# Feed-forward of a two-block transformer kernel: which engine makes the low halves of the input's Winograd forms, and where one down weight is split

## The reference

```python
        h2 = rmsnorm(x, norm2_g[l])
        gate = jnp.einsum('bsd,df->bsf', h2, w_gate[l])
        up = jnp.einsum('bsd,df->bsf', h2, w_up[l])
        x = x + jnp.einsum('bsf,fd->bsd', jax.nn.silu(gate) * up, w_down[l])
    return rmsnorm(x, final_norm_g)
```

## Time and profile before

| | |
|---|---|
| median of 3 runs | 3688.02 us (3686.49 to 3693.86) |
| profiled execution, its own time | 3687.42 us |
| its span in the profile | 3685.7 us |
| TensorE busy | 3505.6 us, 95% |
| VectorE busy | 2130.1 us, 58% |
| GpSimd busy | 1732.3 us, 47% |
| ScalarE busy | 1155.6 us, 31% |

### The profile page before, as it was taken

How to read it: one execution, slowest core, us unless ns; L and a number is a source line. 1 busy time by engine, 2 the same in 40 slices (tenths; PEclk the granted TensorE clock), 3 DMA queues, 4 the chain that set the end, 5 groups by cost and what they waited for, 6 DMA issues and landing times.

```text
span 3685.7 us, 51935 instructions
## 1 busy us (share of the span) xinstructions
PE 3505.6 (95%) x22042; PEld 2927.5 (79%) x22042; DVE 2130.1 (58%) x2745; ACT 1155.6 (31%) x1919; POOL 1732.3 (47%) x1248
## 2 busy tenths in 40 slices
PE   8999999988999999999999999989999899999998
PEld 7788878867778787877878888777788777787876
DVE  7845566377364545456774466647778355454454
ACT  2122122267222222223122122336666222222223
POOL 4332333549255555555233323632488345545454
PEclk9999999999999999999999999999999999999999
DMA  3110312554101111113111132362121200101011
GB/s 124 36 41 30 143 64 83 180 143 143 59 23 46 58 46 58 46 57 143 47 35 35 35 149 80 117 203 70 58 92 58 92 23 35 69 35 69 35 69 63
DMA packets 79690, 275.82 MB, mean 75 GB/s; under 512 B 9057, under 2 KB 9313, under 8 KB 76900
## 3 DMA queue, kind: packets, MB, share of 16 engines
q1 hardware_dynamic: 70816, 242.25, 19.6%
q10 hardware_dynamic: 8642, 30.24, 2.2%
HBM read 224.23 MB, written 48.23 MB: 74 GB/s over the span
## 4 chain that ended last, share of the span: by engine, by line
PE 74%; DVE 15%; ACT 4%; POOL 3%; issue 3%; DMA 0%; POOLq 0%; SPq 0%; DVEq 0%; ACTq 0%
PE ps L1426 20%; PE ps L1428 19%; PE ps L1427 19%; PE ps L1432 4%; PE ps L1726 2%; PE ps L1696 2%; PE ps L1697 2%; PE ps L1731 2%; DVE tf_lo_p L2122 2%; DVE acc L2123 1%; DVE af_hi_p L2122 1%; ACT wd_hi L1780 1%; DVE af_lo_p L2122 1%; DVE px L2122 1%; PE ps L1501 1%
## 5 line engine op out<-in xcount | busy, mean ns | idle before, releaser
L2717 POOL TENSOR_TENSOR ring_lo<-ring_raw,ring_hi 128x512 fp32r<-128x512 f32 (+1 forms) x356 | 596.6, 1681 | 381.8 <-ACT ring_hi L1780 372.2
L1426 PE MATMUL ps<-a_hi,ring_hi 128*128 128x512 f32 x1472 | 589.5, 400 | 29.9 <-DVE af_hi_p L2122 16.0
L1428 PE MATMUL ps<-a_hi,ring_lo 128*128 128x512 f32 x1472 | 575.9, 391 | 0.0
L1427 PE MATMUL ps<-a_lo,ring_hi 128*128 128x512 f32 x1472 | 575.8, 391 | 0.0
L1426 PEld LDWEIGHTS ps<-a_hi,ring_hi 128*128 128x128 f32 x1472 | 277.8, 189 | 104.2 <-DVE af_hi_p L2122 23.6
L1428 PEld LDWEIGHTS ps<-a_hi,ring_lo 128*128 128x128 f32 x1472 | 277.6, 189 | 59.9
L1427 PEld LDWEIGHTS ps<-a_lo,ring_hi 128*128 128x128 f32 x1472 | 278.2, 189 | 54.3
L2122 DVE TENSOR_TENSOR xres<-xres,ps 128x512 f32<-128x512 f32 x352 | 234.6, 684 | 147.9 <-PE ps L1428 145.7
L1426 PE MATMUL ps<-wd_hi,af_hi 128*128 128x512 f32 x704 | 277.0, 394 | 24.5 <-DVE xres L2122 18.7
L1780 ACT ACTIVATE ring_hi<-ring_raw 128x512 fp32r<-128x512 f32 (+1 forms) x286 | 180.6, 635 | 308.8 <-PE ps L1428 195.5
L1427 PE MATMUL ps<-wd_lo,af_hi 128*128 128x512 f32 x704 | 275.8, 392 | 0.0
(11 more groups left out here) (305 smaller groups left out, 8055.6 us busy)
## 6 DMA issues: line engine op xcount, KB each, us to landing
ring_raw<-w SPq DMA_DIRECT2D x92, 512.0 KB, 3.6
ring_raw<-wgu SPq DMA_DIRECT2D x68, 512.0 KB, 3.7
uq<-q_scr SPq DMA_DIRECT2D x96, 256.0 KB, 4.7
ring_raw<-wd SPq DMA_DIRECT2D x34, 512.0 KB, 3.6
ring_raw<-wo SPq DMA_DIRECT2D x32, 512.0 KB, 3.6
uk<-k_scr SPq DMA_DIRECT2D x6, 2048.0 KB, 10.5
rlf<-wgu SPq DMA_DIRECT2D x20, 512.0 KB, 4.5
xraw<-xt SPq DMA_DIRECT2D x16, 512.0 KB, 7.4
```

The lines of the kernel that those rows point to most:

```text
L1426: pe.matmul(o, ah, bh, start=begin and i == 0, stop=False)
L1427: pe.matmul(o, ah, bl, start=False, stop=False)
L1428: last = pe.matmul(o, al, bh, start=False, stop=end and i == len(pairs) - 1)
L2717: tt = lambda o, a, b, op: pool.tensor_tensor(o, a, b, op=op)
```

## The change

In the feed-forward (x = 1) VectorE now makes what GpSimd made of the input's forms: the difference of the low halves in step 0, the low halves of t3, t2 and t4 in steps 2, 4 and 6, and t1's low half; and it makes t1's high half, which ScalarE made. The steps of x = 1 are then the same as those of x = 0. For group 0 alone, the low half of the second down weight (`wd001`) goes from VectorE to GpSimd. The order of the list is the same. The marks that later steps wait for change their engine with the work.

```diff
@@ jobs of the down weights
-                    ("act", ("pool", "dve")[m], "later"), wide=True)
+                    ("act", "dve" if m and g else "pool", "later"), wide=True)
@@ tensor
-                        for mark in new("pe", [("x_lo_dve" if x == 0 else "x_lo_pool", hf, x, p, z)]):
+                        for mark in new("pe", [("x_lo_dve", hf, x, p, z)]):
@@ scalar: removed
-            elif kind == "xform1" and a[1:2] + a[3:] == [1, 2]:
...
-                copy(FORMS[1]["t1"][0][:, ks, :], PLAIN[1]["t1"][1][:, ks, :]).then_inc(*up("x_hi", hf, x, "t1", z))
@@ vector
-                    t = tt(t3l, b22h, b12h, ALU.subtract)
-                    if x == 0:
-                        t = tt(t4h, b22l, b12l, ALU.subtract)
+                    tt(t3l, b22h, b12h, ALU.subtract)
+                    t = tt(t4h, b22l, b12l, ALU.subtract)
...
-                    if x:
-                        for mark in new("dve", [("xform_low", hf, z)]):
-                            dve.wait_ge(*at(*mark))
...
-                if x == 0 and i in (2, 4, 6):
+                if i in (2, 4, 6):
                     p = ("t3", "t2", "t4")[i // 2 - 1]
                     for mark in new("dve", [("x_hi", hf, x, p, z)]):
                         dve.wait_ge(*at(*mark))
...
-                        for mark in new("dve", [("dense", hf, "311", 1), ("x_lo_pool", hf, 1, "t4", z)]):
+                        for mark in new("dve", [("dense", hf, "311", 1), ("x_lo_dve", hf, 1, "t4", z)]):
...
-                    if x == 0:
-                        r1h, r1l = (y[:, ks, :] for y in FORMS[0]["t1"])
...
+                    r1h, r1l = (y[:, ks, :] for y in FORMS[x]["t1"])
+                    for mark in new("dve", [("xform", hf, x, z, 9)]):
+                        dve.wait_ge(*at(*mark))
+                    times(r1h, t1l, 1.0).then_inc(*up("xform", hf, x, z, 10))
+                    for mark in new("dve", [("xform", hf, x, z, 10)]):
+                        dve.wait_ge(*at(*mark))
+                    tt(r1l, t1l, f32(r1h), ALU.subtract).then_inc(*up("x_lo_dve", hf, x, "t1", z))
@@ gpsimd: removed
-            elif kind == "xform" and a[1]:
...
-                    tt(PLAIN[1]["t4"][0][:, ks, :], f32(FORMS[1]["b22"][1][:, ks, :]), f32(FORMS[1]["b12"][1][:, ks, :]),
-                       ALU.subtract).then_inc(*up("xform_low", hf, z))
...
-                    tt(FORMS[1][p][1][:, ks, :], PLAIN[1][p][1][:, ks, :], f32(FORMS[1][p][0][:, ks, :]), ALU.subtract
-                       ).then_inc(*up("x_lo_pool", hf, 1, p, z))
-            elif kind == "xform1" and a[1:2] + a[3:] == [1, 2]:
...
-                tt(r1l, PLAIN[1]["t1"][1][:, ks, :], f32(r1h), ALU.subtract).then_inc(*up("x_lo_pool", hf, 1, "t1", z))
```

More of the change, by code:

```diff
@@ L2856, in gpsimd @@
                 tt(rs, rs, MHALF[:, 0:1].to_broadcast([128, 1]), ALU.pow).then_inc(*up("norm_rms", hf, which, t))
-            elif kind == "xform" and a[1]:
[L2859 to L2864, removed]
-                    tt(PLAIN[1]["t4"][0][:, ks, :], f32(FORMS[1]["b22"][1][:, ks, :]), f32(FORMS[1]["b12"][1][:, ks, :]),
-                       ALU.subtract).then_inc(*up("xform_low", hf, z))
[L2867 to L2873, removed]
-                    tt(FORMS[1][p][1][:, ks, :], PLAIN[1][p][1][:, ks, :], f32(FORMS[1][p][0][:, ks, :]), ALU.subtract
-                       ).then_inc(*up("x_lo_pool", hf, 1, p, z))
-            elif kind == "xform1" and a[1:2] + a[3:] == [1, 2]:
-                hf, x, z, i = a
-                ks = slice(2 * z, 2 * z + 2)
-                r1h, r1l = (y[:, ks, :] for y in FORMS[1]["t1"])
-                for mark in new("pool", [("x_hi", hf, 1, "t1", z)]):
-                    pool.wait_ge(*at(*mark))
-                tt(r1l, PLAIN[1]["t1"][1][:, ks, :], f32(r1h), ALU.subtract).then_inc(*up("x_lo_pool", hf, 1, "t1", z))
             elif kind == "pool_sum":
```

## The result

The changed kernel takes 3696.12 us (median of 12 runs, 3686.69 to 3703.17), the kernel before 3690.04 in the same comparison (12 runs, 3684.44 to 3694.34). The ratio is 1.0016, 95% interval [1.0008, 1.0023]: slower by 0.16%. (Every ratio here is the one that the comparison gave; it is not always the quotient of the medians.) The profiled execution took 3693.44 us, 6.0 more than the profiled one of before.

A forecast was written before the change was run, and what follows sets the result against it. VectorE's queue up to the first addition was taken as the bound: 26.2 + 6.0 + 1.1 + 13.0 = 46.3 us against 43.96, 2.4 later, twice 4.8, giving 3692.8 us; forecast's own range 3690 to 3698, overall 3682 to 3701.

The forecast's parts named there:

- The path: VectorE's stretch from first difference to first addition decides; it was to go from 43.96 to 46.3 us.
- the stop: TensorE's wait for xres before the fifth down product was to grow from 6.9 to 8.3 us, ending 2.4 later.
- The term of VectorE's own work: In VectorE's stretch: 22 instructions, ten at 1.25 us and twelve at 1.14, together 26.2 us.
- Contention, 13.0 us: In VectorE's stretch: waiting inside instructions for what GpSimd still does, 13.0 us against 16.1 before.
- The other waits: In VectorE's stretch: evacuations stay at 6.0 us, a new 1.1 us wait comes, 3.7 us of earlier waits go.
- wait of 1.1 us in step 6 of slice 1: New VectorE wait: step 6 follows step 5 at once and needs ScalarE's rounding of t4.
- The first wait: TensorE's wait for af_lo before group 0's down projection, 1.5 us before, was to be near 2.5 us.
- The slow matmuls after the stop: Low-clock matmuls after TensorE's wait for xres were to stay, costing 2.1 to 2.7 us.
- The additions: VectorE's first addition to the residual was expected near 1091.4 us and, in the second half, near 3045.3.
- t1 hidden under the products: VectorE's added t1 work between additions, 5.6 us up to 7.8, was to be hidden by the slow matmuls.
- Rival A: Shared SBUF access, not VectorE's queue, is the bound: -1.3 us a half, 3685.4 us; chance 0.18.
- Rival B: GpSimd's remaining instructions fall into VectorE's pauses and TensorE's stop closes: 3666.4 us; chance 0.1.

The follow-up runs named there:

- e4: Changed kernel with GpSimd's four sums of group 1's first gate weights run over 8 of 512 columns, leaving work out: 3685.15 us, ratio 0.999.
- e5: Kernel before, old engines, with the t1 (xform1) steps held behind additions 4, 8, 12 and 16: 3688.69 us, ratio 0.9988.
- e6: Changed kernel with the t1 (xform1) steps held behind additions 4, 8, 12 and 16: 3686.81 us, ratio 0.9985.
- e2: Changed kernel with t1's high half back on ScalarE and its low half back on GpSimd: 3694.28 us, ratio 1.0012.
- e9: Changed kernel with only the difference of the low halves back on GpSimd: 3692.41 us, ratio 1.0006.
- e1: Changed kernel with the low half of wd001 back on VectorE: 3700.44 us, ratio 1.0024.
- e7: Changed kernel with slice 1's steps 1 to 6 held between pairs of additions, t1 steps behind them: 3679.53 us, ratio 0.9965.
- e8: Kernel before, old engines, with slice 1's steps 1 to 6 held between pairs of additions, t1 steps behind them: 3676.32 us, ratio 0.9956.
- e11: Changed kernel with slice 1's steps held between additions but placed earlier, t1 after the fifth to eighth: 3672.07 us, ratio 0.9956.
- e10: Kernel before, old engines, with slice 1's steps held between additions but placed earlier, t1 after the fifth to eighth: 3686.19 us, ratio 0.9991.

## Why the prediction was right, step by step

**The path.** VectorE's queue up to the first addition sets when TensorE goes on, in both kernels. e4, e5 and e6 shortened it by 4.1, 2.3 and 4.4 us, and TensorE came to t4 earlier every time: by 4.0 and 3.0 us, 3.5 and 2.0, and 5.5 and 4.4 in the two halves of the sequence. What differs from the queue's gain is the number of slow matmuls behind the stop.

**The term of VectorE's own work** (26.2 us, 22 instructions at 1.25 or 1.14): held. The rows show the same pitches.

**Contention, 13.0 us.** Measured, with each duration in the changed kernel's stretch less its uncontended one: 12.8. By its pieces: 0.73 for the copy (forecast 0.75), 2.0 and 2.2 for the low halves of `gu0011` and `wd000` (2.1 and 2.2), 0.5 for that of `wd001` (0.5), seven meetings at half size of 1.0 to 1.1 (7.3 in all; forecast 7.4).

**The other waits** were 0.7 us too small. The second evacuation waits 1.05 us for ScalarE instead of 0.70: ScalarE was still rounding t4 (the row at 1060.79, which ends at 1061.85) when `af_hi` was due. And four times a low half starts 0.10 us after the end of the sum ahead of it, where 0.03 was usual. Its high half was ready by then (at 1074.85 for over a microsecond), so the cause isn't shown. Forecast 46.3 us, measured 46.8: this, less the 0.2 by which contention was put too high, is the difference. Of the wait of 1.1 us in step 6 of slice 1, 1.12 was there.

**The first wait and the stop.** The first wait was put at about 2.5 us and is 2.68. The stop was to grow to 8.3 and is 7.1 and 6.8. Here a step failed that cost nothing: I kept the four products at full clock, but after 2.68 us of idleness they ran partly at the lower level and took up 1.3 us of the stop. The moment at which it ends is the forecast's, 0.5 us off. The slow matmuls after the stop, 13 and 8, were put at the 13 and 10 of the kernel before. The forecast had no means to tell this number (last section); that it came so near is luck.

**The additions.** The first was expected near 1091.4 us and 3045.3, and came at 1091.58 and 3049.69. The second is off by 4.4 us. The forecast put it 2.4 later than before and forgot that the first half, by the same sum, had already moved it by 2.4. Of the other 2.0, 0.5 are the second stretch itself (46.83 us for 46.3), and the rest came between the two first additions.

**t1 hidden under the products:** held, with no wait of TensorE from the fifth product on, and by e2.

**The total.** Forecast 0.13% more, measured 0.16% [0.08%, 0.23%]; forecast 4.8 us for the two halves, measured 4.9 by the stage and 5.1 by t4. The forecast's 3692.8 us for the median was counted from the median of three executions, 3688.02; beside the changed kernel the one before had 3690.04, so 2.0 of the 3.3 us to the measured 3696.12 are the starting point's.

**Rival A**, the shared access as the bound, would have shortened the stretch by 1.3 us. It grew by 2.9, and e9 (49.1 by that rule, 45.63 measured) and e1 (longer with the instruction on VectorE, not shorter) speak against it as well. The lock itself is real. VectorE's full-size subtraction takes 3.25 to 3.40 us beside a full-size low half of GpSimd, and one that reads PSUM stays at 0.68. The Trainium skill, "SBUF — State Buffer", section "Who interferes with whom", calls it exclusive; that agrees, and from it alone one would have concluded the wrong sign.

**Rival B**, the stop closes, needed contention under 3 us. It was 12.8. e7 and e8 closed both stops by another way, the order, with 13 and 16 us less by their medians, not the 21.6 that B gave: waits at t3 and t1 took their place.

## What to carry over

The shares of GpSimd and VectorE before (47% and 58%) didn't say which way this move would go: count what the receiving queue holds between the last moment at which it is free and the instruction that others wait for, and take from it only the contention that the moved work had caused, here 1 us for each meeting at half size and 2 at full size, less whatever of the other engine moves up into the gap. Before moving work ask whether it must stand ahead of the awaited instruction at all: the best order tried was worth 16.2 us of stage on the old engines (e8) and 19.6 on the new (after to e11), the move itself 4.9. But an order is good only for the queues it was made for: e8's gave 15.4 on the new engines (e7), e11's only 4.5 on the old (e10). With an order that suits it the changed kernel (e11, ratio 0.9956 [0.9944, 0.9969]) is level with the best on the old engines (e8, the same ratio and interval), and both beat the two kernels of this case.

## What the runs showed of the hardware

**The clock after waits.** The number of slow matmuls didn't follow the length of the wait alone. In this stage of the thirteen traces, TensorE's waits of over 1 us and the slow matmuls (over 0.55 us) that came behind each:

| wait, us | how many | slow matmuls behind it |
|---|---|---|
| 1.05 to 1.64 | 12 | none |
| 1.77 to 1.89 | 4 | none (two), 8 (two) |
| 2.44 to 2.71 | 8 | none (one), 6 to 8 |
| 3.03 to 3.40 | 6 | none (one), 6 to 14 |
| 4.59 to 8.47 | 16 | 6 to 13 |

The same kernel falls to either side at the same wait: e10 after 1.80 us in the first half of the sequence (three matmuls fast, then eight slow) and 1.77 in the second (none), e11 after 1.89 both times (eight, none), e1 after 3.35 and 3.33 (seven, none). What decides it isn't shown. Each slow matmul costs about 0.2 us, so eight of them or none make 1.6 us behind a single wait. TensorE's timelines of e10 for the first half and then the second:

```profile
1092.04 0.50 PE L1436 MATMUL ps<-wd_hi,af_hi 128*128 128x512 f32 x1 [1.80 <-DVE xres L2132]
...
1093.23 0.63 PE L1437 MATMUL ps<-wd_lo,af_hi 128*128 128x512 f32 x1
...
3042.81 0.50 PE L1436 MATMUL ps<-wd_hi,af_hi 128*128 128x512 f32 x1 [1.77 <-DVE xres L2132]
...
3044.30 0.39 PE L1436 MATMUL ps<-wd_hi,af_hi 128*128 128x512 f32 x1
```

**Each engine is held for the length of the other's instruction.** VectorE's 128 x 1024 subtraction, 1.22 us alone, lost 2.0 to 2.2 us beside full-size instructions of GpSimd, 1.0 to 1.1 beside half-size ones and nothing that shows beside e4's sums over 8 columns. Those sums still took 3.46 us for three, over 1.1 each: they stood waiting for VectorE's instructions. So it is the short instruction that pays, and shortening GpSimd's frees VectorE without making GpSimd's stream much faster.

**Low-clock episodes outside the edited work.** e10 and e11 are 14.1 us apart by their medians and 14.5 by the spans of their profiled executions, but 10.2 by the stages. The rest lies between 880 and 985 us, ahead of everything that differs: TensorE waits alike in both there (12.4 and 13.6 us in all, the longest 3.1), but the granted clock was 0.93 in e10 and 0.98 in e11, which took e10 from 0.4 to 4.7 us behind. So an episode stands behind a wait here too, and the same wait has one in one execution and not in the other.
